# Latent and context passes of a split-precision product interleaved one by one in a two-stream transformer trunk

## The reference

```
def swiglu(h, wg, wu, wd):
    return (jax.nn.silu(h @ wg) * (h @ wu)) @ wd

def ffn_sublayer(s, m, i, g, wg, wu, wd):
    h = modulate(rmsnorm(s, g), m[3 * i], m[3 * i + 1])
    return s + 0.5 * m[3 * i + 2] * swiglu(h, wg, wu, wd)
...
x = ffn_sublayer(x, mx, 0, ...)      # 512 x 1024, all four blocks
ctx = ffn_sublayer(ctx, mc, 0, ...)  # 256 x 1024, three of the four blocks
```

## Time and profile before

| | |
|---|---|
| median of 3 runs | 2925.57 us (2925.35 to 2925.83) |
| span of the profiled execution, first to last instruction | 2926.3 us |
| mean granted TensorE clock over the span | 0.977 of full speed |
| PE busy | 2776.4 us, 95% of the span, 15304 matmuls |
| PEld busy | 2337.2 us, 80% |
| DVE, ACT, POOL busy | 59%, 27%, 6% |
| DMA | 255.33 MB, mean 87 GB/s |

### The profile page before, as it was taken

The page is one execution under the profiler, slowest core; times in us unless marked ns, Lnnn a source line. Parts: engine busy times, 40 slices in busy tenths (PEclk is TensorE's granted clock), DMA queues, the critical chain, the costliest instruction groups (busy, mean ns, idle before and its releaser), DMA issues.

```text
span 2926.3 us, 37875 instructions
## 1 busy us (share of the span) xinstructions
PE 2776.4 (95%) x15304; PEld 2337.2 (80%) x15304; DVE 1721.8 (59%) x2313; ACT 777.4 (27%) x1078; POOL 176.6 (6%) x136
## 2 busy tenths in 40 slices
PE   5899999999987899999999999999999987999998
PEld 3688888879955688888888788888888845888887
DVE  3655565664966655565555765556346776544445
ACT  3211211223136532121111311121124146322223
POOL 1000000020011120000000300000012010200001
PEclk8899999999999999999999999999999999999999
DMA  7523232221101013233332232323121101123221
GB/s 260 174 100 115 86 119 96 87 87 58 44 29 44 15 58 124 93 100 108 101 107 72 72 121 97 113 86 123 50 73 58 58 29 58 56 102 101 86 86 44
DMA packets 180706, 255.33 MB, mean 87 GB/s; under 512 B 5266, under 2 KB 128764, under 8 KB 180604
## 3 DMA queue, kind: packets, MB, share of 16 engines
q1 hardware_dynamic: 180604, 253.90, 26.0%
HBM read 251.78 MB, written 2.10 MB: 87 GB/s over the span
## 4 chain that ended last, share of the span: by engine, by line
PE 86%; DVE 6%; ACT 3%; POOL 2%; issue 1%; DMA 1%; SPq 0%; ACTq 0%; POOLq 0%; DVEq 0%
PE ps L798 26%; PE ps L799 26%; PE ps L800 26%; PE ps L1135 2%; POOL sqsum L790 1%; PE ps L1057 1%; PE ps L1163 1%; DVE h_lo L1586 1%; DVE tn L1575 1%; ACT w_hi L1237 1%; DVE hsq L1919 1%; PE ps L1149 1%; DVE e L1935 1%; DVE e L1933 1%; PE ps L931 1%
## 5 line engine op out<-in xcount | busy, mean ns | idle before, releaser
L798 PE MATMUL ps<-h_hi,w_hi 128*128 128x512 f32 (+1 forms) x3040 | 1049.0, 345 | 21.5 <-DVE w_lo L1559 10.8
L799 PE MATMUL ps<-h_lo,w_hi 128*128 128x512 f32 (+1 forms) x3040 | 1048.0, 345 | 0.0
L800 PE MATMUL ps<-h_hi,w_lo 128*128 128x512 f32 (+1 forms) x3040 | 1040.4, 342 | 0.0
L798 PEld LDWEIGHTS ps<-h_hi,w_hi 128*128 128x128 f32 x3040 | 578.6, 190 | 98.3 <-DVE w_lo L1559 10.5
L800 PEld LDWEIGHTS ps<-h_hi,w_lo 128*128 128x128 f32 x3040 | 576.1, 190 | 72.0
L799 PEld LDWEIGHTS ps<-h_lo,w_hi 128*128 128x128 f32 x3040 | 578.2, 190 | 67.3 <-issue 1.0
L1684 DVE TENSOR_TENSOR prod<-sil,ps 128x512 f32<-128x512 f32 (+1 forms) x156 | 82.6, 565 | 664.1 <-PE ps L800 657.7
L798 PE MATMUL ps<-hid_hi,w_hi 128*128 128x512 f32 (+1 forms) x1248 | 431.1, 345 | 0.0
L800 PE MATMUL ps<-hid_hi,w_lo 128*128 128x512 f32 (+1 forms) x1248 | 429.7, 344 | 0.0
L799 PE MATMUL ps<-hid_lo,w_hi 128*128 128x512 f32 (+1 forms) x1248 | 427.7, 343 | 0.0
L1237 ACT ACTIVATE w_hi<-raw 128x2048 fp32r<-128x2048 f32 x158 | 297.0, 1906 | 444.3 <-PE ps L800 440.6
(11 more groups left out here) (135 smaller groups left out, 2043.3 us busy)
## 6 DMA issues: line engine op xcount, KB each, us to landing
side_raw<-in_w_ada SPq DMA_DIRECT2D x116, 512.0 KB, 3.6
raw<-in_w_ffn_gate SPq DMA_DIRECT2D x44, 1024.0 KB, 5.1
raw<-in_w_ffn_up SPq DMA_DIRECT2D x44, 1024.0 KB, 5.1
raw<-in_w_ffn_down SPq DMA_DIRECT2D x44, 1024.0 KB, 4.8
raw<-in_w_ada SPq DMA_DIRECT2D x14, 1024.0 KB, 8.6
raw<-in_w_in SPq DMA_DIRECT2D x14, 1024.0 KB, 5.1
raw<-in_w_out SPq DMA_DIRECT2D x8, 1024.0 KB, 6.6
raw<-in_w_in SPq DMA_DIRECT2D x8, 512.0 KB, 4.5
```

The lines of the kernel that those rows point to most:

```text
L798: mm(out, wh, xh, start=start, stop=False)
L799: mm(out, wh, xl, start=False, stop=False)
L800: return mm(out, wl, xh, start=False, stop=stop)
```

## The change

A new helper `mm3_over` takes a list of banks and a list of activation pieces and runs the three passes over both streams: high by high for the latent and then the context columns, then the second pass for both, then the third. In `gate_up` and in the `down` of groups 0 to 9 it takes the place of `mm3`. The matmuls are the same in number, shape and operands, and each bank still gets its passes in the same order. In `down` the waits for both banks of an output block now stand ahead of the block's first pass, and both banks are completed one behind the other at its end. `gate_up_first`, the last group's down product and all products of the mixing stage still use `mm3`. In block 3 there is one stream, and the order is what it was.

```
+        def mm3_over(outs, wh, wl, xs, start, stop):
+
+            done = []
+            for i, (w, lo) in enumerate(((wh, False), (wh, True), (wl, False))):
+                for out, (xh, xl) in zip(outs, xs):
+                    done.append(mm(out, w, xl if lo else xh, start=start and i == 0, stop=stop and i == 2))
+            return done[2 * len(outs):]
...
                             for k in range(KD):
-                                for s, (o, n) in enumerate(ss):
-                                    last = mm3(pt((w, f, g, c, s), n), wh[:, k, 128 * c:128 * c + 128],
-                                               wl[:, k, 128 * c:128 * c + 128], h_hi[:, k, o:o + n], h_lo[:, k, o:o + n],
-                                               k == 0, k == KD - 1)
+                                for last in mm3_over([pt((w, f, g, c, s), n) for s, (o, n) in enumerate(ss)],
+                                                     wh[:, k, 128 * c:128 * c + 128], wl[:, k, 128 * c:128 * c + 128],
+                                                     [(h_hi[:, k, o:o + n], h_lo[:, k, o:o + n]) for o, n in ss],
+                                                     k == 0, k == KD - 1):
                                     if k == KD - 1:
                                         last.then_inc(products, 1)
...
                     for j in range(KD):
-                        for s, (o, n) in enumerate(ss):
+                        for s in range(len(ss)):
                             wait_bank(pe, lambda x: ("d", f, x, j, s), g, it)
-                            for c in range(2):
-                                last = mm3(pt(("d", f, g, j, s), n), wh[:, c, 128 * j:128 * j + 128],
-                                           wl[:, c, 128 * j:128 * j + 128], hid_hi[:, g % 2, c, o:o + n],
-                                           hid_lo[:, g % 2, c, o:o + n], c == 0, c == 1)
-                            last.then_inc(products, 1)
+                        for c in range(2):
+                            for last in mm3_over([pt(("d", f, g, j, s), n) for s, (o, n) in enumerate(ss)],
+                                                 wh[:, c, 128 * j:128 * j + 128], wl[:, c, 128 * j:128 * j + 128],
+                                                 [(hid_hi[:, g % 2, c, o:o + n], hid_lo[:, g % 2, c, o:o + n]) for o, n in ss],
+                                                 c == 0, c == 1):
+                                if c == 1:
+                                    last.then_inc(products, 1)
```

## The result

| | median us | runs |
|---|---|---|
| before, on the same chip | 2925.7 | 2925.35 to 2933.64 |
| changed | 2944.14 | 2940.15 to 2944.38 |

The ratio is 1.0053, 95% interval 1.0039 to 1.0068: the change makes the kernel slower by about half a per cent. The profiled execution of the changed kernel has a span of 2942.6 us, 16.3 more than before.

The account below looks back on a forecast made before the run. PE, busy 95% of the span and never stopped in the touched loops, was taken to bound the kernel. The terms +1.9 - 1.4 = +0.5 us on 2925.6 gave 2926 us, range 2909 to 2943.

Parts of the forecast that it names:

- The likeliest case: Whole kernel: unit spacing kept within 4.1 ns either way, time within 0.2%, 2920 to 2932 us; chance 0.40.
- PE's spacing is all that can move the time, and no wait appears: Touched loops: PE is never stopped there, so only pass spacing or a wait not there yet could move the time.
- Order in `gate_up`, +1.9 us: gate_up of blocks 0 to 2: unit goes from 1050 to 1052 ns, +2 ns on 960 units.
- The first reading: gate_up: what ran before a pass sets its spacing; every latent pass 226.7 + 9 ns, every context pass 120 - 5.
- surplus at every change of length: Slower rival: latent passes pay 9 ns each, context passes get no refund; +22 us, 2948 us, half 2937; chance 0.27.
- Four passes on one stationary block save nothing: gate_up: four passes on one stationary operand instead of two save nothing by repetition, 0 us.
- Order in `down`, -1.4 us: down of blocks 0 to 2: -3 ns on 480 units, a quarter of mixing's gain, bounds -12 to +12 ns.
- Moved bank wait and late completion, 0 us: Earlier second-bank wait in down has 1.5 us of cover; later bank completion in gate_up and down delays nothing; 0 us.
- Even spacing: Faster rival: strict alternation as regular as lone forms, gate_up -9.6 us, down -4.8 us, 2911 us; chance 0.31.

Follow-up runs that it names:

- e10: The changed kernel once more, for a second profile: 2941.9 us against 2926.58 for the kernel before, ratio 1.0049.
- e1: Only the gate and up products interleaved, down products as in the kernel before: 2938.05 us against 2928.25, ratio 1.0038.
- e8: Kernel before with long runs in gate_up, down two output blocks at a time, feed-forward tiles shifted 128 bytes: 2920.46 us, ratio 0.9969.
- e6: The full change with the feed-forward tiles shifted 128 bytes in SBUF: 2935.03 us against 2929.24 for the kernel before, ratio 1.0019.
- e11: The full change with context pass ahead of latent in every pair except the one completing a product: 2929.01 us against 2926.58 before, ratio 1.0011.
- e4: The full change with the third interleaved pass using the high weights, so one stationary block per unit: 2944.44 us against 2928.25 before, ratio 1.0052.
- e2: Only the down products interleaved, with their moved bank wait, gate_up as in the kernel before: 2929.62 us against 2928.25, ratio 1.0005.
- e9: The kernel before once more, unchanged, for a second profile: 2926.62 us, ratio 1.000.
- e5: Kernel before with hidden activations and other feed-forward tiles placed 128 bytes further in SBUF: 2929.98 us against 2929.24, ratio 1.0006.
- e12: e5 once more, for a second profiled execution: 2929.69 us against 2925.58 for the kernel before, ratio 1.0006.

## Why the prediction was right and where it failed

The range was 2909 to 2943 us, counted from 2925.6. On that base the measured ratio gives 2941.1 us, and e10's median is 2941.9, both near the upper end; the median of the first measurement, 2944.1, lies 1 us above it. The likeliest case, no change, did not come, and the range held by the width that a rival gave it, not by the forecast's mechanism. The touched loops give 11.5 us of the slowdown; the rest, which carried it to the edge, was in no term of the prediction. Point by point.

- *PE's spacing is all that can move the time, and no wait appears.* Right for the part that the loops measure: they take 11.5 us more with PE busy throughout, and no wait is new. About 4 to 7 us more lie outside them (last point).
- *Order in `gate_up`, +1.9 us.* This is the step that failed. It measured +9.6 us (960 x 10 ns), e1 +9.8 by its medians. The first reading said that a pass's spacing is set by the neighbour behind it, 398 ns for all latent and 278 for all context passes. Latent passes came at 397, 395 and 403, so that half was about right. Context passes came at 278, 281 and 284: only one in three kept the refund that the reading gave to all three. By the spacings the latent passes of a unit pay 30 ns over the lone form where the reading said 27, and the context passes give back 10 where it said 15. The time is that of the rival "surplus at every change of length" in a little over half its size, near the 2937 us that the text names; its full size, no refund at all, would have been +17 a unit.
- Behind it stood a wrong idea of the effect. The passes don't answer to their neighbours one by one. The second latent pass, slow behind another latent one, was in the text as an objection to the reading, and it was the clue: the spacing of latent passes needs five to settle after a change of length, as e8's run shows, and an alternating sequence settles into a rhythm of its own. e6, e11 and one group of e1 show two such rhythms, and which of them comes can't be read off the durations in the earlier trace rows.
- *Four passes on one stationary block save nothing.* Right, and e4 shows it for six.
- *Order in `down`, -1.4 us.* Wrong sign, small: +1.4 by e2's median, about 4 ns a unit by the profiles (12.73 us against 12.68 for six output blocks). The bounds of 12 ns either way held.
- *Moved bank wait and late completion, 0 us.* Right, by e2.
- *Even spacing*, 2911 us: not in the changed kernel's two profiles, yet half of the groups of e6's first block, a quarter of each group of e11 and one group of e1 run at its time. Its 2911 us took -10 ns a unit for `down` too, where the prediction's own sum of the lone forms, 1061, lies 12 above the mixed unit.
- *What is left.* The medians differ by 18.4 and 15.3 us (e10), e1 and e2 together give 11.2, the loops 11.5. About 4 to 7 us are in stages that the change leaves alone; in the two shown, the attention of either layer, the longer time comes with a lower mean clock (0.91 for 0.93, 0.90 for 0.92). Over the whole span the clock does not set the kernels apart: e10's mean is 0.975, and so is e9's. e5 with e12 and e9 show stages wandering by 1 to 2.4 us each with one and the same program. Yet it is no accident of one run: all 12 runs with both products interleaved in the order of the change and at its places (the first measurement, e10, e4) lie between 2940.2 and 2946.6 us. Why these stages come out longer behind the changed loops stays open.

## What to carry to other kernels

Where PE is never idle, the order of passes still has a price: in this kernel it paid to put passes of the same length next to each other, and to change the length rarely. Going from 2 changes in six passes to 2 in 48 gained 0.2%, going to one at every pass in the gate and up products cost 0.4%. The second is no fixed price of a change: in its even rhythm the alternating sequence was as fast as the long runs (33.28 us a group against 33.36), but no experiment could choose the rhythm. With effects this small, compare the time of one repeated group in the profiles, which repeats to a hundredth of a microsecond, before trusting medians that scatter by several.

## What the runs showed of the hardware

- At 2.4 GHz, three-pass matmuls in the rounded float32 type space out at 226.7 ns for 512 columns and 120.0 ns for 256, each among its own kind, for more than 50 passes on end (gate and up products). Behind a change of length the first five of 512 columns take 229 to 236 ns, the first of 256 columns 113 and the second 119 (e8).
- The same alternating instructions ran 32 units at 1.040 us each in one group and at 1.060 in the next (e6). Both rhythms came without the shift of the tiles too: in e11 inside one group, in e1 in block 0's first.
- Moving the streamed tile by 128 bytes in its partition took lone latent passes of `down` from 233.6 to 227 ns (e5, both profiles). Only this one shift was tried.
- Why the spacing of lone passes has these values, and what decides between the rhythms, is open: e4 rules out the identity of the loaded block; e5 shows that the place of the tiles has a part in the spacing of lone passes, and e11 that the rhythm can turn where one pair is exchanged.
